# Layer 1 round seams, layer 2 mixer order and early decays in a two-layer float32 kernel on one core

## The reference, cut to what matters

```python
u = jnp.einsum('bsd,dn->bsn', h, w_in)                       # h = rms_norm(x, g_pre)
y_pool = pool_mixer(pool_v, pool_w, pool_scale) * silu(pool_g)
y_conv = conv_mixer(conv_x, conv_gb, conv_gc, conv_w, conv_b) * silu(conv_g)
y_sb = stick_breaking_attention(sb_q, sb_k, sb_v) * silu(sb_g)   # 8 heads of 64
merged = jnp.sum(gates * proj, axis=2)                       # proj: each y by its w_branch
x = x + rms_norm(merged @ w_out, g_post)
```

```python
att = swa_sink_alibi(a_q, a_k, a_v, sinks)                   # window of 128 tokens, 4 heads
ssd = ssd_mixer(s_z, s_xbc, s_dt, ...)                       # state-space scan, 8 heads
gdn = gdn_mixer(g_qkv, g_z, g_b, g_a, ...)                   # gated delta rule, 4 heads
mix = jnp.concatenate([att, ssd, gdn], -1) @ w_out
x = x + rmsnorm(mix); f = (silu(h @ w_gate) * (h @ w_up)) @ w_down; x = x + rmsnorm(f)
```

## Time and profile before

| | |
|---|---|
| median of 3 runs | 2770.74 us (2764.66 to 2772.31) |
| profiled execution | 2769.36 us, its span 2767.4 us |
| mean granted TensorE clock | 0.972 of full speed |
| PE busy | 2557.6 us, 92% |
| DVE, ACT, POOL busy | 1383.3, 954.9, 383.5 us |

### The profile page before, as it was taken

One profiled execution on the slowest core, in us unless ns is written; L12 is line 12 of the kernel. 1 busy time (PEld: TensorE's weight loads), 2 busy tenths in 40 slices (PEclk: granted clock), 3 DMA queues, 4 the chain that ended last, 5 costly groups with the idle time before them and its releaser, 6 DMA issues. The chain is left out here.

```text
span 2767.4 us, 34204 instructions
## 1 busy us (share of the span) xinstructions
PE 2557.6 (92%) x12420; PEld 2110.3 (76%) x12420; DVE 1383.3 (50%) x1618; ACT 954.9 (35%) x1599; POOL 383.5 (14%) x377
## 2 busy tenths in 40 slices
PE   7999999987999999999995888787999999999996
PEld 5887878776888887878785777776877777777774
DVE  4665666565332324545314676674644444444446
ACT  4766676775221112322212333333311111111112
POOL 0332323332000000000003344340000000000002
PEclk9999999998999999999998999999999999999998
DMA  3011110101121213312222101002231111111111
GB/s 128 31 47 40 38 62 31 55 31 61 61 76 53 76 46 103 109 63 91 106 99 89 46 23 44 24 0 93 105 129 45 46 45 45 45 45 49 49 52 62
DMA packets 69572, 169.41 MB, mean 61 GB/s; under 512 B 5616, under 2 KB 31600, under 8 KB 69488
## 3 DMA queue, kind: packets, MB, share of 16 engines
q1 hardware_dynamic: 69488, 168.40, 17.8%
HBM read 136.92 MB, written 31.46 MB: 61 GB/s over the span
## 5 line engine op out<-in xcount | busy, mean ns | idle before, releaser
L81 DVE TENSOR_TENSOR w_lo<-w_raw,w_hi 128x1024 fp32r<-128x1024 f32 x164 | 207.1, 1263 | 606.9 <-ACT w_hi L76 606.5
L76 ACT CAST w_hi<-w_raw 128x1024 fp32r<-128x1024 f32 x166 | 174.1, 1049 | 715.5 <-PE psG L52 315.8
L52 PE MATMUL psG<-h_hi,w_hi 128*128 128x512 f32 x1408 | 348.8, 397 | 15.0 <-ACT w_hi L76 6.5
L52 PE MATMUL psG<-h_lo,w_hi 128*128 128x512 f32 x1408 | 340.7, 391 | 0.0
L52 PE MATMUL psG<-h_hi,w_lo 128*128 128x512 f32 x1408 | 340.0, 390 | 0.0
L52 PEld LDWEIGHTS psG<-h_hi,w_hi 128*128 128x128 f32 x1408 | 269.1, 192 | 73.1 <-issue 10.7
L52 PEld LDWEIGHTS psG<-h_lo,w_hi 128*128 128x128 f32 x1408 | 264.8, 189 | 55.2
L52 PEld LDWEIGHTS psG<-h_hi,w_lo 128*128 128x128 f32 x1408 | 263.4, 188 | 55.1 <-DVE w_lo L81 0.3
L1982 DVE TENSOR_TENSOR features_T<-features_T,ff_o 128x1024 f32<-128x1024 f32 x176 | 212.8, 1219 | 29.3 <-PE ff_o L52 23.3
L52 PE MATMUL psH<-h_ffn_hi,w_hi 128*128 128x512 f32 x704 | 168.2, 391 | 2.6 <-PEq L873 2.6
L52 PE MATMUL psH<-h_ffn_lo,w_hi 128*128 128x512 f32 x704 | 167.8, 390 | 0.0
(11 more groups left out here) (352 smaller groups left out, 4267.8 us busy)
## 6 DMA issues: line engine op xcount, KB each, us to landing
w_raw<-in_units SPq DMA_DIRECT2D x182, 512.0 KB, 3.4
features<-p_res SPq DMA_DIRECT2D x24, 512.0 KB, 2.6
m_feat<-features SPq DMA_DIRECT2D x8, 1536.0 KB, 6.9
y_branches<-features_T SPq DMA_DIRECT2D x12, 512.0 KB, 4.1
mg_y<-y_branches SPq DMA_DIRECT2D x3, 2048.0 KB, 10.6
n_x<-in_x SPq DMA_DIRECT2D x8, 512.0 KB, 8.1
o_x<-in_x SPq DMA_DIRECT2D x8, 512.0 KB, 3.4
x_layer<-o_x SPq DMA_DIRECT2D x8, 512.0 KB, 2.6
```

The lines of the kernel that those rows point to most:

```text
L52: return pe.matmul(out, lhs, rhs, start=first, stop=last, skip_group_check=True)
L76: act.copy(self.hi[c % 2][:] if dest is None else dest, self.raw[c % 2][:]).then_inc(self.hi_done, 1)
L81: dve.tensor_tensor(self.lo[c % 2][:] if dest is None else dest, self.raw[c % 2][:], hi.bitcast(F32), ALU.subtract).then_inc(self.lo_done, 1)
```

## The change

Three things change. (1) In layer 1 the left-over steps move into the next round: a new function `ending(i, s)` on ACT, DVE and PE is called at steps 0 to 2 of round i+1 for round i. The transposes of V stand after the first step's projections, and their evacuation is done in two halves (`turned_v` and `turn_v` with `h`). The attention's store follows the first unit load of the next round. POOLV is projected before SBG. Round 0 and round 3 are written out, and rounds 1 and 2 are a loop. (2) In layer 2's mixers ACT's copies `product(16)` and `product(32)` and the copy `mtg` come earlier, DVE's `xdt`, `xdec` and `sd` come earlier, and POOL starts `m_nm` when DVE has done `vt1`, no longer at `nt`. (3) The decays are computed inside `layer2_projections`, between the last units; parameter rows, masks, biases and 20 of 24 feature blocks of tile 0 are loaded there too, and the last four are loaded at the start of the mixers' block (`f_late`).

```diff
@@ layer1_mixers: tensor @@
-                def iteration(i, nu):
+                def turn_values(i):
                     entry_free(pe, U0, i)
                     entry_out(pe, 2, i)
...
+                def ending(i, s):
+                    if s == 0:
+                        sums(i, NS - 1)
+                    values(i, NS - 2 + s)
+
+                def iteration(i, nu, first=False):
                     for s in range(NS):
                         logits(i, s)
                         projections(i, *groups(nu)[s])
+                        if s == 0:
+                            turn_values(i)
+                        if s < 2 and not first:
+                            ending(i - 1, s)
                         if s >= 1:
                             sums(i, s - 1)
...
-                    sums(i, NS - 1)
-                    values(i, NS - 2)
-                    values(i, NS - 1)
@@ layer1_mixers: scalar (vector alike) @@
+                def ending(i, s):
+
+                    if s < 2:
+                        weights(i, NS - 2 + s)
+                    if s == 0:
+                        high_parts(i, NS - 1)
+                    if s == 2:
+                        move_out(i, 3)
...
+                        if not first:
+                            ending(i - 1, s)
+                        if s == 2:
+                            turned_v(i, 1)
...
                         softplus_parts(i, s)
+                        if s == 0:
+                            turned_v(i, 0)
@@ layer1_mixers: sync @@
+                    for j in range(loads):
+                        W.load(sp, U0 + 2 + j, UI, i)
+                        if j == 0 and not first:
+                            store_attention(i - 1)
@@ layer2_projections @@
+                all_units(act, body, after_silu=decays_front, after_plain=decays_back)
...
+                all_units(dve, body, small_columns, decays_front, decays_middle, decays_back)
...
+                all_units(pe, body, small_columns, turn_small, after_plain=decay_sums)
@@ layer2_mixers @@
-                sp.dma_start(F[:], feats[:, :, 0:P].rearrange("c p t -> p c t")).then_inc(f_here, 16)
-                sp.dma_start(MSK[:], masks).then_inc(c_here, 16)
...
+                for s in range(2):
+                    sp.wait_ge(D2.stored[s], 16 * (N_FEAT // 2))
+                sp.dma_start(F[:, AQ0:, :], feats[AQ0:, :, 0:P].rearrange("c p t -> p c t")).then_inc(f_late, 16)
...
-                        vectF.wait(g, "nt", n)
+                        vectF.wait(g, "vt1", n)
...
+                        pe.wait_ge(f_late, 16)
                         turn(tensF, "tr4", 4, [F[:, c] for c in (GZ0, GZ0 + 1, AV0)])
```

More of the change, by code:

```diff
@@ L258, in layer1_mixers, with done_before @@
         NL = [sum(kb > 0 for _, _, kb in STEPS[:s]) for s in range(NS + 1)]
+        def done_before(n, i, s):
+            return n * NS * i + n * s if not isinstance(i, int) or i else max(n * s, 0)
         def first_query(s):
@@ L313, in store, with store_attention, iteration @@
                     sp.dma_start(y_out[NC4 + i], y[1]).then_inc(y_stored[1], 16)
+                def store_attention(i):
                     sp.wait_ge(o_gated, 4 * i + 4)
                     sp.dma_start(y_out[2 * NC4 + i], y[2]).then_inc(y_stored[2], 16)
+                def iteration(i, loads, first=False):
+                    start(i)
+                    for j in range(loads):
+                        W.load(sp, U0 + 2 + j, UI, i)
+                        if j == 0 and not first:
+                            store_attention(i - 1)
+                    store(i)
                 for c in range(2, 5):
                     W.load(sp, c)
[L319 to L327, removed]
+                iteration(0, UI, True)
+                with sp.Fori(1, NC4 - 1) as i:
+                    iteration(i, UI)
+                iteration(NC4 - 1, SECTIONS)
+                store_attention(NC4 - 1)
                 for b in range(3):
@@ L600, in iteration @@
                             gate_out(i, GROUP_END.index(s - 3))
+                        if not first:
+                            ending(i - 1, s)
+                        if s == 2:
+                            turn_v(i, 1)
                         if s >= 2:
@@ L1035, in all_units @@
             after_two()
[L1036 to L1043, removed]
+            with eng.Fori(1, CONV // 2) as i:
+                for s in range(2):
+                    body("conv", s, 2, i)
+            after_conv()
+            with eng.Fori(0, SILU // 2) as i:
+                for s in range(2):
+                    body("silu", CONV + s, 2, i)
+            after_silu()
+            for c in range(CONV + SILU, N_FEAT):
+                body("plain", c, 0, 0)
+                if c == CONV + SILU:
+                    after_plain()
         with nc.Block() as block:
@@ L1254, in layer2_mixers @@
-def layer2_mixers(nc, C, feats, rows, prm, masks, attn_bias, mixT):
+def layer2_mixers(nc, C, feats, D2, mixT):
     with ExitStack() as ctx:
@@ L1416, in tile @@
                         scalF.done("sq", a.activation(SQ[:], QK[:], ACT.Square))
+                    if t is not None:
+                        tensH.wait(a, "mtrg", t)
+                        scalH.done("mtg", a.copy(mixT[:, 6:8, bass.ds(t * P, P)], PS[:, 2, 0:256].rearrange("p (c t) -> p c t", c=2)))
                     if chain:
@@ L1570, in tile @@
                         vectF.done("sdif", tt(sdif[:], row("sinks", AH), mx[:], ALU.subtract))
+                        scalF.wait(v, "L", n)
+                        tensF.wait(v, "sc", n)
+                        for g in range(2):
+                            vectF.done(f"sd{g}", tt(SD[:, 4 * g:4 * g + 4], DEC[:, 4 * g:4 * g + 4],
+                                                    over(PS[:, 0, P * g:P * g + P], 4), ALU.mult))
                     level(32)
```

309 lines of the change are left out of this document (156 added, 153 removed).

## The result

The changed kernel takes 2690.08 us in the median (2686.57 to 2695.01, four runs), beside 2771.52 us for the kernel before (2764.66 to 2777.13, four runs). The ratio is 0.9709, with a 95% interval of 0.9681 to 0.9736, so the change saves about 81 us, between 73 and 88 by the interval; 73 were forecast. The profiled executions stand at 2769.36 and 2686.57 us, 82.8 us apart.

A forecast was written before the change was run, and what follows sets the result against it. Layer 1's rounds were taken as bound by PE, losing only at their ends, and layer 2's mixers as a chain of waits. 18 + 19 + 36 = 73 us off gave 2697 us in the median's terms, range 2672 to 2724.

The forecast's parts named there:

- Seams, 18 us: Layer 1's round seams: PE's stalls and slow starts go, 20.9 us less charges, net 18 us, bounds 12 and 21.
- The margins: Layer 1's seams: `sb_sp_lo` ready at 5.3 us against 5.8 on PE; step 2's `psG0` wait charged 0.5 us at two seams.
- The 1 us charged to the left-over sums of the last round: Layer 1's last round: 14 projections in a step, so the cover for `sb_sp_lo` is gone; 1 us charged.
- Boundary, 19 us: Between layer 2's projections and mixers: early decays and loads make the decay sums earlier, net 19 us, bounds 15 and 21.
- the matmuls inserted into PE's stream: Layer 2's projections: two decay matmuls and the small transposes now run in PE's stream, about 1.3 us more.
- the late load: Start of layer 2's mixers: `tr4` waits for the load of four feature blocks, taken as 2.5 us between nothing and 6.5.
- Mixers, 36 us: Layer 2's mixers: 4.9 us in each of seven tiles and about 1.5 in the first, 36 us in sum.
- step (e): Layer 2's mixer tile: from X64 and `VT64` to the tile's end the chain is the old one.
- the loss I had named as a lower bound: Layer 2's mixers: POOL's later copies push on DVE's tail by up to 1.5 us a tile, 10 us less; taken as zero.
- A wait on POOL: Sign of being wrong: a wait on POOL on PE's or DVE's side in layer 2's mixers.
- the clock, the term set to nothing: Layer 2's mixers: granted clock 0.94, about 12% at 1.2 GHz, 47 us; no change taken, 10 us either way.
- the rivals: Mixers short 2717 (0.13), new waits at seams 2708 (0.07), late load 2701 (0.03), slower or nothing (0.03).

The follow-up runs named there:

- `boundary_only`: Kernel before with only the second part: decays, parameters and first tile's features within layer 2's projections; 2753.66 us beside 2770.60, ratio 0.9943.
- `act_back`: Changed kernel with ACT's copies of T16 and T32 back behind the wide exp and the score exps; 2731.22 us, ratio 0.9846.
- `act_only`: Changed kernel with all of the mixers' reordering undone except ACT's two earlier copies (T16, T32); 2696.45 us, ratio 0.9714.
- `dve_back`: Changed kernel with DVE's `sd`, `xdt` and `xdec` back in the tail of the tile; 2694.74 us, ratio 0.9716.
- `pool_nt`: Changed kernel with POOL's masks starting at DVE's `nt` again, not at `vt1`; 2694.41 us, ratio 0.9715.
- `bias_once`: Changed kernel with POOL's copy of the 128x1024 bias made in the first tile alone; 2690.62 us, ratio 0.9698.
- `pool_tail`: As `bias_once`, with ACT's `mtg` copy back behind the group norm and POOL's `gzn` behind `qgt` and `qkdc`; 2696.02 us, ratio 0.9714.

## Why the prediction held, term by term

**Seams, 18 us.** Right. The changed kernel's merge starts at 664.78 instead of 684.11, 19.3 us earlier. Eleven of the traces here hold these seams: four start the merge at 664.5 to 664.9 and seven at 668.5 to 669.9; three without them at 684.1 to 686.0. The mean gain is 17.5, so some of the 19.3 is the luck of the profiled execution. The margins were judged well in size: 0.53 us at step 2 of two rounds where I charged 0.5. The 1 us charged to the left-over sums of the last round was misplaced: they find their input ready at 522.56, as in the other rounds, and the last round waits 1.53 us two steps later, for the low part of step 1.

**Boundary, 19 us.** Right: 18.9 us alone in the trace and 16 by the runs of `boundary_only`, 19.3 in the changed kernel up to the decay sums, 20.8 behind them. Of the single terms, the matmuls inserted into PE's stream cost nothing that shows, where I charged 1.3 us (the merge starts 19.33 us earlier, the last projection pass 19.29), and the late load 2.9 us from its issue to PE's next transposes where I took 2.5.

**Mixers, 36 us.** The mechanism held, and its size came out 5 us short through two errors of opposite sign. From the decay sums' end to the last turn of `m_mix` the stage gained 41.1 us. A tile at full clock gained 4.2 us, not 4.9: the term that was mis-sized is step (e), the tail that was to stay as it was. Up to T2 a tile is 5.05 us shorter, as said; then `m_oss` (0.76 instead of 0.17) and `ym` (2.27 instead of 1.49) give back most of a microsecond, since POOL's masks start later and its next copies fall beside them. That is the loss I had named as a lower bound and set to zero. The rule on which I set it, of the Trainium skill's page "SBUF — State Buffer", section "Who interferes with whom", held as far as it went: the masks are faster beside PSUM-reading operations, 7.41 against 9.21 us, though not the 6 to 7 forecast. The prediction left out a condition of that section of the Trainium skill: it exempts an instruction with at most one SBUF input only outside the two-port modes. `m_oss` has one such input and is slowed; in which mode it ran no run here shows. A wait on POOL, named as a sign of being wrong, does not show beyond 0.19 us a tile on DVE, which the kernel before has as well (put down to DVE there). Seven tiles at 4.2 and the first at 0.7 are 30 us. The other 11 are left to the clock, the term set to nothing: 0.98 in place of 0.94. Of them 6.5 are read from tiles: above six tiles at full clock the kernel before spends 9.7 us, the changed kernel 3.2. The forecast of the stage is near the measured one partly by luck, since this gain made up for the tail. No single edit brings the clock back: `act_back` shows that it takes ACT's copies, and `act_only` that they are not enough. For `mtg` nothing was forecast, and it is nothing in the runs (2689.50 against 2690.08 us), while the traces have a tile at full clock 0.4 us shorter without it.

Of the rivals none came true. What I could have read beforehand is that two of the six tiles before, at full clock, took 47.27 us and the four with slow stretches 48.6 to 50.9: slow stretches already cost 9.7 us in six tiles whose waits were to go, so the bound of 10 us for the clock should have leaned to one side.

## What to carry to other kernels

Where a chain goes through an in-order engine, look first for the short copy that stands behind long independent work on it: moving two copies of 0.6 us was worth 40 us here, and without them the other edits of the stage left the mean tile where it was (48.91 against 48.89 us). Where one stage's tail needs no new data, put it behind the next stage's first independent matmuls, and count the engines' hand-overs to see that it is ready in time. When waits go, price the clock that they cost too, from tiles with and without a slow stretch. And compare tiles at the same clock: the mean alone hid the loss of `dve_back` and made one of `act_only`.

## What was new of the hardware

The same wait need not cost the same. In the last round of layer 1 the changed kernel and `pool_nt`, whose code is the same there, wait 2.5 us before one matmul; in one the clock stays, in the other it falls. Ahead of it `pool_nt` is 0.56 us behind, at the next low part 1.94: 1.4 us hang on this wait. Another such difference, behind 629 us, adds 1.5, and at the merge `pool_nt` is 3.7 us behind. First the changed kernel, then `pool_nt` with its window from 518.5 to 650 us:

```profile
585.58 0.50 PE L705 MATMUL psA<-sb_sp_lo,minus_from_r 128*128 128x512 f32 x1 [2.46 <-DVE sb_sp_lo L539]
```

```profile
586.14 0.79 PE L705 MATMUL psA<-sb_sp_lo,minus_from_r 128*128 128x512 f32 x1 [2.48 <-DVE sb_sp_lo L539]
```

```profile
518.50:650.00 131.50, 119.49 (x541) 96.53 (x540) 78.40 (x118) 95.33 (x188) 48.89 (x50) 0.96 0.09 33
```

The changed kernel has 0.99 in that window. Why the one is spared stays open.

A small DVE operation beside POOL is not slowed in proportion to its size. `m_oss`, on four numbers a lane, takes 0.17 us in the kernel before, 0.76 in the changed kernel, 0.56 in `bias_once` and 1.73 in `dve_back`. In the last three it ends within 0.04 us of the end of the POOL instruction beside which it started (1645.79 and 1645.77 in the changed kernel), and so does `m_yss` in `pool_tail`. DVE and then POOL in `dve_back`, which end at 1608.13 and 1608.10:

```profile
1606.40 1.73 DVE L1691 TENSOR_SCALAR m_oss<-m_oss 128x4 f32<-128x4 f32 x1
```

```profile
1606.21 1.89 POOL L47 TENSOR_TENSOR m_bias<-m_bias_rest,m_zero 128x1024 f32<-128x1024 f32 x1
```

So what such an operation loses here is what is left of POOL's instruction when it starts. This holds for the ones looked at, not for every small operation: `RECIPROCAL` takes 0.18 us at 1639.07, in the midst of POOL's masks.
